# Neighbourhood and windowed attention in float32 halves: the low key product on 64 rows, scores of both heads of a tile in one step

## The chip, the cores and the metric

The program runs on 1 core of one Trainium2 chip. The metric is the device time of one execution in microseconds (us), taken as the median over runs. Engines are named as in the profile: PE is TensorE's matmuls, PEld its weight loads, DVE is VectorE, ACT is ScalarE, POOL is GpSimd, SP is SyncE, which issues most transfers.

## The reference, cut to what matters

One encoder layer over 2048 tokens of width 1024: normalise, one input projection, two groups of attention heads, an output projection, a SwiGLU feed-forward part and a last norm. All is float32. The change touches the scores `q . k` of both groups:

```
# A: 8 heads, a query sees a window of 8 x 16 neighbours in a grid of 32 x 64 tokens
logits = einsum(qb, kb) * scale + bias ; masked ; softmax ; @ vb
# B: 8 query heads over 2 key heads, |q - k| <= 128, with a sink logit
logits = einsum(qb, kb) * scale ; masked ; softmax with sink ; @ vb
# a head has 64 dimensions, so a score is a sum over 64 products
```

## The kernel before

**Stages.** The stages follow each other on PE: the input projection, attention, the output projection with its norms ("mix"), and the feed-forward part.

**Halves.** PE multiplies operands of type float32r in one pass at reduced precision. Where full precision is wanted, the projection stores each of q and k as a high and a low float32r half (`stage_hi`, `stage_lo`, to `qk_scratch`), and a product takes high x high, low x high and high x low. A head's 64 dimensions fill only half of the 128 rows of PE's array. So `q_st` holds for each head e of a pair the high half of q on rows 0 to 63 and its low half on rows 64 to 127. `k_st[:, e, 0]` holds the high half of the keys twice, on both halves of the rows, and `k_st[:, e, 1]` the low half twice. One unit's scores are two matmuls into one PSUM bank: L985 gives (q_hi + q_lo) x k_hi, and L986 adds (q_hi + q_lo) x k_lo. Both use all 128 rows, and both load the same weights, `q_st[:, e, tile]`.

**Order.** Attention has 8 rounds, 4 of the neighbourhood kind ("near") and 4 of the window kind. A round is two heads over all 2048 queries. It has 16 tiles of 128 queries and 32 units, and unit u is head e = u % 2 of tile t = u // 2. Key columns of one unit: near tiles 384 (8 of 16 tiles) or 512 (the other 8); window tiles 384, and 256 for the first and last tile of a round. The order on each engine is written out by `stream`: in each step s every stage runs for unit s minus its lag, and what is listed first comes first in the step:

- PE: `score` (lag 0), `turn` (lag 5: 3 or 4 transposes of the probabilities, L997), `values` (lag 7: probabilities x values, L1017, for one tile after its odd unit in window rounds, for two tiles after every fourth unit in near rounds)
- DVE: `invert` (lag 2, L938), `shift` (lag 0: scores plus bias with the running minimum, out of PSUM, L932), `normalise` (lag 2, L945), `results` (L959, after every 8 units)
- ACT: `copy_turned` (lag 5, L906), `set_sinks`, `exp` (L884)

So on PE a step is: two score matmuls, three or four transposes, and in some steps a group of value matmuls. The scores have 4 PSUM banks (`SC_BUFS`): `score(u)` waits until `shift(u - 4)` has read the bank. The transposes and the scores address the array as 128 rows x 128 columns; each value matmul has 64 output columns (128\*64), and the two heads of a tile use the two column halves.

**Transfers.** SP's `advance` loads the next round's q, k and v in four blocks b, each when the round's units 0 to 8(b + 1) - 1 are scored, and stores the results between them. `load_q` (L727) issues 2 transfers for each block, `load_k` (L737) 4, `load_v` 1, `store` (L756) 1. Window rounds load k and v once, since all four rounds share them. The first round's q and k are loaded during the projection (`load_first_q`, `load_first_k`, one call for each step of the projection). GpSimd makes the biases of the next near round and, in the window rounds, scales and splits the output projection's weights (`make_bias`, `gpsimd`).

Of the kernel before, what the change touches and what calls it, by code (L numbers as in the profile page):

```python
# [29 lines left out]
F32R = mybir.dt.float32r  # L30

P = 128
BANK = 512
D = 1024
S = 2048
HD = 64
GW = 64
NAH, SWH, SWKV = 8, 8, 2
# [8 lines left out]
HEADS = 2 * NAH + SWH + SWKV  # L47
# [11 lines left out]
def project_phase(nc, x, g_mix, w_in, rpb, cos2, sin2, ident_in, zeros_in, qk_dram, v_near_dram, v_win_dram,  # L59
# [159 lines left out]
    def load_ahead(att, i):  # L219
# [8 lines left out]
        if i in (3, 4):  # L228
# [3 lines left out]
            att.load_first_q(i - 3)  # L232
        if 7 <= i < 11:
            sp.wait_ge(proj_done, done + 7)
            att.load_first_k(i - 7)
# [387 lines left out]
def attention_phase(nc, qk_dram, v_near_dram, v_win_dram, rel_dram, near_mask_in, win_mask_in, sink_in, ident_in, o_dram, mem,  # L623
# [17 lines left out]
    def sem(n):  # L641
        return nc.alloc_semaphore(f"att_{n}")

    q_st, k_st, v_sb, sn, pr, pt, pt_low, o_st = (mem.q_st, mem.k_st, mem.v_sb, mem.sn, mem.pr, mem.pt, mem.pt_low,
                                                  mem.o_st)
    negmax, total, rtotal = mem.att_stats
# [63 lines left out]
    def f32(ap):  # L710
        return ap.bitcast(F32)
# [8 lines left out]


    def load_q(kind, r, b):

        qs = slice(b * BANK, (b + 1) * BANK)
        pair = bass.ds(2 * r, 2) if kind.near else bass.ds(2 * NAH - NEAR_ROUNDS + r, 2, SWH // SWKV)
        for part in range(2):
            sp.dma_start(f32(q_st[part * HD:(part + 1) * HD, :, qs]), heads[part, :, pair, qs]) \  # L727
                .then_inc(q_in[b], 16)

    def load_k(kind, r, b):  # L730

        lo, hi = kind.portions[b]
        ks = slice(lo * kind.unit, hi * kind.unit)
        pair = bass.ds(NAH + 2 * r, 2) if kind.near else slice(2 * NAH + SWH, HEADS)
        for part in range(2):
            for twice in range(2):
                sp.dma_start(f32(k_st[twice * HD:(twice + 1) * HD, :, part, ks]), heads[part, :, pair, ks]) \  # L737
                    .then_inc(k_in[b], 16)

# [31 lines left out]
    def load_first_q(part):  # L771

        pair = slice(0, 2)
        sp.dma_start(f32(q_st[part * HD:(part + 1) * HD, :, :]), heads[part, :, pair, :]).then_inc(q_in[0], 16)
        if part == 1:
            for b in range(1, 4):
                sp.sem_inc(q_in[b], 32)

    def load_first_k(piece):

        part, twice = piece // 2, piece % 2
        sp.dma_start(f32(k_st[twice * HD:(twice + 1) * HD, :, part, :]), heads[part, :, NAH:NAH + 2, :]) \
            .then_inc(k_in[0], 16)
        if piece == 3:
            for b in range(1, 4):
                sp.sem_inc(k_in[b], 64)

# [185 lines left out]
    def score(proj, kind, r, u):  # L973
        e, t = u % 2, u // 2
        b, n = t // 4, kind.chunks(t) * P
        if e == 0:
            if t % 4 == 0:
                pe.wait_ge(q_in[b], 32 * (r + 1))
            for i in kind.new_portions(t):
                pe.wait_ge(k_in[i], 64 * (r + 1) if kind.near else 64 * (NEAR_ROUNDS + 1))  # L980
        if isinstance(r, int) and r == 0 and u < SC_BUFS:
            proj.bank_free(pe, u)
        pe.wait_ge(shifted, UNITS * (r + 1) - SC_BUFS + u + 1)
        q, out = q_st[:, e, t * P:(t + 1) * P], sc[:, u % SC_BUFS, 0:n]
        pe.matmul(out, q, kind.keys(k_st[:, e, 0, :], t), start=True, stop=False)  # L985
        pe.matmul(out, q, kind.keys(k_st[:, e, 1, :], t), start=False, stop=True).then_inc(scored, 1)  # L986

# [48 lines left out]
class Memory:  # L1036
# [11 lines left out]
    def __init__(self, nc):  # L1048
# [8 lines left out]
        self.q_st = self.at("att_q_stack", 65536, [P, 2, S], F32R)  # L1057
        self.k_st = self.at("att_k_stack", 81920, [P, 2, 2, S], F32R)
        self.v_sb = self.at("att_values", 114688, [P, 32, P])
# [1164 lines left out]
```

## Time and profile before

| | us |
|---|---|
| median of 3 runs (2261.32 to 2263.62) | 2262.09 |
| the profiled execution's own time | 2259.97 |
| its span, from the first to the last instruction | 2258.2 |
| PE busy | 2208.8 (98% of the span) |
| PEld busy | 1818.5 (81%) |
| DVE busy | 1440.5 (64%) |
| ACT busy | 922.3 (41%) |
| POOL busy | 327.8 (15%) |

Matmuls are pipelined: each takes several times as long as the next one is behind it. A busy share of PE near 100% therefore only says that PE rarely stood with an empty array, and not that it works at its peak. What a matmul costs is read from the distance between the end of one and the end of the next. The granted TensorE clock is 0.996 of full speed on average. Attention takes the stretch from 442 to about 769 us; the last score matmul starts at 764 us.

### The profile page before, as it was taken

Reading aid. Unit: us, or ns where it says so; the run is one execution under the profiler, and the core shown is the slowest. Engines: PE = TensorE matmul, PEld = TensorE weight load, DVE = VectorE, ACT = ScalarE, POOL = GpSimd, SP = SyncE. Lnnn points to the kernel's source line nnn. Section 1 sums busy time; section 2 is a strip of 40 time slices with the busy share of each in tenths; the row PEclk is TensorE's granted clock in tenths of the full one; section 3 lists DMA queues with packets and bytes.
Section 4 is the critical chain, followed back from the end, with each engine's and each line's share of the span. In section 5 each row is a group of like instructions: output and inputs, shape, how many; then the busy total and the mean of one; then the engine's idle time right before and its main releaser. Section 6 shows DMA issues by size and latency. Waiting matters only on the chain.

```text
span 2258.2 us, 33189 instructions
## 1 busy us (share of the span) xinstructions
PE 2208.8 (98%) x11464; PEld 1818.5 (81%) x11464; DVE 1440.5 (64%) x2747; ACT 922.3 (41%) x1824; POOL 327.8 (15%) x304
## 2 busy tenths in 40 slices
PE   7999999999999999999999999999999999999998
PEld 6888888788877788778888887888888877888886
DVE  4412143399899777776666657665656578565776
ACT  4411121288888633343333334433333333131342
POOL 3370001145334100011212120000000002020100
PEclk9999999999999999999999999999999999999999
DMA  6472425789954275675545457323232286353544
GB/s 225 140 186 99 140 87 148 201 217 246 235 143 111 83 226 200 224 265 175 189 165 199 154 209 263 128 80 131 80 131 73 102 305 234 104 177 108 191 145 152
DMA packets 274677, 376.68 MB, mean 167 GB/s; under 512 B 15258, under 2 KB 182306, under 8 KB 269168
## 3 DMA queue, kind: packets, MB, share of 16 engines
q1 hardware_dynamic: 266528, 354.15, 49.3%
q0 software_dynamic: 5568, 11.87, 2.0%
q10 hardware_dynamic: 2448, 8.91, 1.4%
q8 instruction: 81, 1.33, 0.2%
q14 instruction: 52, 0.43, 0.1%
HBM read 237.77 MB, written 140.31 MB: 167 GB/s over the span
## 4 chain that ended last, share of the span: by engine, by line
PE 89%; DVE 6%; DMA 2%; issue 2%; ACT 1%; POOL 0%; DVEq 0%; ACTq 0%; SPq 0%
PE late_psum L2047 11%; PE late_psum L2048 11%; PE late_psum L2049 11%; PE late_psum L2078 6%; PE late_psum L2080 5%; PE late_psum L2079 5%; PE late_psum L1017 4%; PE late_psum L997 4%; PE late_psum L527 3%; PE late_psum L528 3%; PE late_psum L529 3%; PE late_psum L555 3%; PE late_psum L554 3%; PE late_psum L556 3%; PE late_psum L985 2%; PE late_psum L1396 2%
## 5 line engine op out<-in xcount | busy, mean ns | idle before, releaser
L2047 PE MATMUL late_psum<-ff_h,ff_ring 128*128 128x512 f32 x1232 | 479.9, 390 | 5.9 <-DVE ff_acts L1907 3.0
L2049 PE MATMUL late_psum<-ff_h,ff_ring 128*128 128x512 f32 x1232 | 479.3, 389 | 0.0
L2048 PE MATMUL late_psum<-ff_h,ff_ring 128*128 128x512 f32 x1232 | 479.3, 389 | 0.0
L2047 PEld LDWEIGHTS late_psum<-ff_h,ff_ring 128*128 128x128 f32 x1232 | 231.2, 188 | 55.9 <-DVE ff_h L1868 3.9
L2049 PEld LDWEIGHTS late_psum<-ff_h,ff_ring 128*128 128x128 f32 x1232 | 231.2, 188 | 48.1
L2048 PEld LDWEIGHTS late_psum<-ff_h,ff_ring 128*128 128x128 f32 x1232 | 231.2, 188 | 47.7
L2078 PE MATMUL late_psum<-ff_d,ff_a 128*128 128x512 f32 x616 | 240.6, 391 | 8.3 <-DVE ff_x L1967 5.3
L2079 PE MATMUL late_psum<-ff_d,ff_a 128*128 128x512 f32 x616 | 239.7, 389 | 0.0
L2080 PE MATMUL late_psum<-ff_d,ff_a 128*128 128x512 f32 x616 | 239.7, 389 | 0.0
L1967 DVE TENSOR_TENSOR ff_x<-late_psum,ff_x 128x512 f32<-128x512 f32 x224 | 153.6, 689 | 121.4 <-PE late_psum L2080 121.0
L1863 DVE TENSOR_TENSOR ff_ring<-ff_raw,ff_ring 128x512 fp32r<-128x512 f32 x176 | 127.5, 726 | 104.3 <-ACT ff_ring L1740 104.1
L884 ACT ACTIVATE att_probs<-att_neg_scores,att_negmax 128x385 f32<-128x385 f32 (+3 forms) x256 | 163.9, 640 | 27.4 <-DVE att_negmax L932 24.4
L1863 DVE TENSOR_TENSOR ff_ring<-ff_sums,ff_ring 128x512 fp32r<-128x512 f32 x132 | 96.4, 732 | 114.9 <-ACT ff_ring L1740 114.5
L1755 ACT CAST ff_a<-ff_a 128x768 fp32r<-128x768 f32 (+2 forms) x96 | 81.6, 879 | 209.6 <-DMA ff_a<-acts_scratch 209.6
L1740 ACT CAST ff_ring<-ff_raw 128x512 fp32r<-128x512 f32 x176 | 109.6, 624 | 140.8 <-PE late_psum L2049 137.6
L2078 PEld LDWEIGHTS late_psum<-ff_d,ff_a 128*128 128x128 f32 x616 | 115.6, 188 | 35.5 <-issue 4.3
L945 DVE TENSOR_SCALAR att_probs<-att_probs,att_rtotal 128x384 f32<-128x384 f32 (+2 forms) x256 | 143.5, 560 | 0.1
L1708 POOL TENSOR_TENSOR ff_d<-ff_d 128x1536 fp32r<-128x1536 f32 x9 | 35.7, 3962 | 727.7 <-ACT ff_d L1749 727.7
L997 PE MATMUL late_psum<-ident,att_probs 128*128 128x128 f32 x816 | 132.4, 275 | 7.1 <-DVE att_probs L945 3.0
L2080 PEld LDWEIGHTS late_psum<-ff_d,ff_a 128*128 128x128 f32 x616 | 115.6, 188 | 24.3
L2079 PEld LDWEIGHTS late_psum<-ff_d,ff_a 128*128 128x128 f32 x616 | 115.7, 188 | 23.6
L833 POOL TENSOR_TENSOR bias<-near_mask,rel 128x384 f32<-128x384 f32 (+1 forms) x72 | 84.9, 1213 | 319.6 <-DMA near_mask<-in_na_mask 198.0
(159 smaller groups left out, 4148.9 us busy)
## 6 DMA issues: line engine op xcount, KB each, us to landing
acts_scratch<-ff_acts SPq DMA_DIRECT2D x22, 1792.0 KB, 7.8
ff_a<-acts_scratch SPq DMA_DIRECT2D x24, 960.0 KB, 5.1
ff_raw<-in_w_gate SPq DMA_DIRECT2D x44, 512.0 KB, 3.8
ff_raw<-in_w_up SPq DMA_DIRECT2D x44, 512.0 KB, 3.9
ff_d<-down_scratch SPq DMA_DIRECT2D x21, 768.0 KB, 6.3
att_q_stack<-qk_scratch SPq DMA_DIRECT2D x56, 256.0 KB, 5.2
ffn_in_scratch<-mix_h_stage SPq DMA_DIRECT2D x8, 1792.0 KB, 6.2
ff_h<-ffn_in_scratch SPq DMA_DIRECT2D x14, 1024.0 KB, 7.6
```

The costliest lines, as they stand in the source:

```text
L884: nc.scalar.activation(pr[:, i, lo:hi], sn[:, i, lo:hi], ACT.Exp, bias=negmax[:, i:i + 1], scale=-1.0, accum_out=total[:, i:i + 1]).then_i ...
L945: nc.vector.tensor_scalar(pr[:, i, c0:c0 + n], pr[:, i, c0:c0 + n], rtotal[:, i:i + 1], None, ALU.mult).then_inc(probs_done, 1)
L997: last = pe.transpose(tp[:, u % 2, j * P:(j + 1) * P], pr[:, i, c0 + j * P:c0 + (j + 1) * P], ident[:])
L1740: nc.scalar.copy(ff.ring[m % TURNS][:, 0], weight_of(m)).then_inc(w_hi_done, 1)
L1863: nc.vector.tensor_tensor(ff.ring[m % TURNS][:, 1], weight_of(m), ff.ring[m % TURNS][:, 0], ALU.subtract) \
L1967: nc.vector.tensor_tensor(to, down_bank(e, j), to, ALU.add).then_inc(added, 1)
L2047: pe.matmul(out_bank, whi[:, k], hhi[:, :, k], start=(k == 0 and not onto), stop=False, skip_group_check=onto)
L2048: pe.matmul(out_bank, whi[:, k], hlo[:, :, k], start=False, stop=False, skip_group_check=onto)
L2049: last = pe.matmul(out_bank, wlo[:, k], hhi[:, :, k], start=False, stop=(k == 3), skip_group_check=onto)
L2078: pe.matmul(bank, hi, dhi, start=(i == 0 and not onto), stop=False, skip_group_check=onto)
L2079: pe.matmul(bank, hi, dlo, start=False, stop=False, skip_group_check=onto)
L2080: last = pe.matmul(bank, lo, dhi, start=False, stop=(i == n - 1), skip_group_check=onto)
```

## The change

The low half of the keys is stacked by head: `k_lo` holds it once, head 0 on rows 0 to 63 and head 1 on rows 64 to 127. The high half is kept twice as before, as `k_hi`. The q stack of head 1 is turned over (low half on rows 0 to 63, high half on rows 64 to 127), so that q's high half lies on the rows of that head's low keys (`half_of`). The low product is now q_hi x k_lo alone, on 64 rows; the product of the two low halves, which the 128-row matmul also gave, is dropped. `score` does nothing for odd units, and for an even unit issues four matmuls: high products of head 0 and head 1 (128 rows), then low products of head 0 (rows 0 to 63) and head 1 (rows 64 to 127), each pair of products into its own bank. It waits for `shift(u - 3)` where before it waited for `shift(u - 4)` and then, a step later, for `shift(u - 3)`. `load_q` issues 4 transfers of half the size for each block, `load_k` 3 in place of 4, and the first loads change in the same way.

```diff
--- before.py
+++ after.py
@@ -230,7 +230,7 @@
             for half in range(2):
                 sp.wait_ge(stored[half], 16 * QK_STEPS)
             att.load_first_q(i - 3)
-        if 7 <= i < 11:
+        if 7 <= i < 10:
             sp.wait_ge(proj_done, done + 7)
             att.load_first_k(i - 7)
         if 11 <= i < 15:
@@ -641,8 +641,8 @@
     def sem(n):
         return nc.alloc_semaphore(f"att_{n}")
 
-    q_st, k_st, v_sb, sn, pr, pt, pt_low, o_st = (mem.q_st, mem.k_st, mem.v_sb, mem.sn, mem.pr, mem.pt, mem.pt_low,
-                                                  mem.o_st)
+    q_st, k_hi, k_lo, v_sb, sn, pr, pt, pt_low, o_st = (mem.q_st, mem.k_hi, mem.k_lo, mem.v_sb, mem.sn, mem.pr, mem.pt,
+                                                        mem.pt_low, mem.o_st)
     negmax, total, rtotal = mem.att_stats
     win_mask, sinks, gcol, w_raw, ident, w_pool = mem.win_mask, mem.sinks, mem.gcol, mem.w_raw, mem.ident, mem.w_pool
     rel, masks, biases = mem.rel, mem.masks, mem.biases
@@ -719,23 +719,28 @@
 
 
 
+    def half_of(part, e):
+
+        row = (part + e) % 2 * HD
+        return slice(row, row + HD)
+
     def load_q(kind, r, b):
 
         qs = slice(b * BANK, (b + 1) * BANK)
-        pair = bass.ds(2 * r, 2) if kind.near else bass.ds(2 * NAH - NEAR_ROUNDS + r, 2, SWH // SWKV)
         for part in range(2):
-            sp.dma_start(f32(q_st[part * HD:(part + 1) * HD, :, qs]), heads[part, :, pair, qs]) \
-                .then_inc(q_in[b], 16)
+            for e in range(2):
+                head = bass.ds(2 * r + e, 1) if kind.near else bass.ds(2 * NAH - NEAR_ROUNDS + r + SWH // SWKV * e, 1)
+                sp.dma_start(f32(q_st[half_of(part, e), e:e + 1, qs]), heads[part, :, head, qs]).then_inc(q_in[b], 16)
 
     def load_k(kind, r, b):
 
         lo, hi = kind.portions[b]
         ks = slice(lo * kind.unit, hi * kind.unit)
         pair = bass.ds(NAH + 2 * r, 2) if kind.near else slice(2 * NAH + SWH, HEADS)
-        for part in range(2):
-            for twice in range(2):
-                sp.dma_start(f32(k_st[twice * HD:(twice + 1) * HD, :, part, ks]), heads[part, :, pair, ks]) \
-                    .then_inc(k_in[b], 16)
+        both = bass.ds((NAH + 2 * r) * HD, P) if kind.near else slice((2 * NAH + SWH) * HD, HEADS * HD)
+        for twice in range(2):
+            sp.dma_start(f32(k_hi[twice * HD:(twice + 1) * HD, :, ks]), heads[0, :, pair, ks]).then_inc(k_in[b], 16)
+        sp.dma_start(f32(k_lo[:, ks]), qk_dram[1, both, ks]).then_inc(k_in[b], 16)
 
     def load_v(kind, r, b):
         lo, hi = kind.portions[b]
@@ -770,20 +775,20 @@
 
     def load_first_q(part):
 
-        pair = slice(0, 2)
-        sp.dma_start(f32(q_st[part * HD:(part + 1) * HD, :, :]), heads[part, :, pair, :]).then_inc(q_in[0], 16)
+        for e in range(2):
+            sp.dma_start(f32(q_st[half_of(part, e), e, :]), heads[part, :, e, :]).then_inc(q_in[0], 16)
         if part == 1:
             for b in range(1, 4):
-                sp.sem_inc(q_in[b], 32)
+                sp.sem_inc(q_in[b], 64)
 
     def load_first_k(piece):
 
-        part, twice = piece // 2, piece % 2
-        sp.dma_start(f32(k_st[twice * HD:(twice + 1) * HD, :, part, :]), heads[part, :, NAH:NAH + 2, :]) \
-            .then_inc(k_in[0], 16)
-        if piece == 3:
-            for b in range(1, 4):
-                sp.sem_inc(k_in[b], 64)
+        if piece < 2:
+            sp.dma_start(f32(k_hi[piece * HD:(piece + 1) * HD, :, :]), heads[0, :, NAH:NAH + 2, :]).then_inc(k_in[0], 16)
+            return
+        sp.dma_start(f32(k_lo[:]), qk_dram[1, NAH * HD:(NAH + 2) * HD, :]).then_inc(k_in[0], 16)
+        for b in range(1, 4):
+            sp.sem_inc(k_in[b], 48)
 
     def load_first_v(b):
         load_v(NEAR, 0, b)
@@ -971,19 +976,25 @@
                {1: proj.last_low}, {UNITS + NORM_LAG - 1: lambda: mix.o_low(0)})
 
     def score(proj, kind, r, u):
-        e, t = u % 2, u // 2
+
+        if u % 2:
+            return
+        t = u // 2
         b, n = t // 4, kind.chunks(t) * P
-        if e == 0:
-            if t % 4 == 0:
-                pe.wait_ge(q_in[b], 32 * (r + 1))
-            for i in kind.new_portions(t):
-                pe.wait_ge(k_in[i], 64 * (r + 1) if kind.near else 64 * (NEAR_ROUNDS + 1))
+        if t % 4 == 0:
+            pe.wait_ge(q_in[b], 64 * (r + 1))
+        for i in kind.new_portions(t):
+            pe.wait_ge(k_in[i], 48 * (r + 1) if kind.near else 48 * (NEAR_ROUNDS + 1))
         if isinstance(r, int) and r == 0 and u < SC_BUFS:
             proj.bank_free(pe, u)
-        pe.wait_ge(shifted, UNITS * (r + 1) - SC_BUFS + u + 1)
-        q, out = q_st[:, e, t * P:(t + 1) * P], sc[:, u % SC_BUFS, 0:n]
-        pe.matmul(out, q, kind.keys(k_st[:, e, 0, :], t), start=True, stop=False)
-        pe.matmul(out, q, kind.keys(k_st[:, e, 1, :], t), start=False, stop=True).then_inc(scored, 1)
+            proj.bank_free(pe, u + 1)
+        pe.wait_ge(shifted, UNITS * (r + 1) - SC_BUFS + u + 2)
+        q, out = [q_st[:, e, t * P:(t + 1) * P] for e in range(2)], [sc[:, (u + e) % SC_BUFS, 0:n] for e in range(2)]
+        for e in range(2):
+            pe.matmul(out[e], q[e], kind.keys(k_hi[:, e, :], t), start=True, stop=False)
+        for e in range(2):
+            rows = half_of(0, e)
+            pe.matmul(out[e], q[e][rows], kind.keys(k_lo[rows], t), start=False, stop=True).then_inc(scored, 1)
 
     def turn(proj, kind, r, u):
         i, t = u % SN_BUFS, u // 2
@@ -1055,7 +1066,8 @@
         self.biases = [self.at(f"bias{i}", off, [P, 2, 3, w]) for i, off, w in ((0, 16896, 384), (1, 28672, 512), (2, 40960, 384))]
         self.pt_low = self.at("att_probs_turned_low", 54784, [P, 4, BANK])
         self.q_st = self.at("att_q_stack", 65536, [P, 2, S], F32R)
-        self.k_st = self.at("att_k_stack", 81920, [P, 2, 2, S], F32R)
+        self.k_hi = self.at("att_k_high", 81920, [P, 2, S], F32R)
+        self.k_lo = self.at("att_k_low", 98304, [P, S], F32R)
         self.v_sb = self.at("att_values", 114688, [P, 32, P])
         self.sn = self.at("att_neg_scores", 131072, [P, 8, BANK])
         self.pr = self.at("att_probs", 147456, [P, 8, BANK])
```

## Rows read from the trace of the kernel before

**Rows 1.** Busy us by stage: PE, PEld, DVE, ACT, POOL; clock, DMA share, GB/s.

```profile
450.00:606.00 156.00, 152.83 (x1447) 127.17 (x1448) 143.69 (x495) 137.10 (x360) 74.43 (x65) 0.98 0.98 237
606.00:766.00 160.00, 156.45 (x1467) 127.18 (x1463) 152.19 (x554) 138.07 (x438) 56.80 (x34) 1.00 0.45 120
766.00:2258.20 1492.20, 1464.97 (x6548) 1208.74 (x6546) 1004.56 (x1407) 537.62 (x834) 102.46 (x53) 1.00 0.49 169
```

**Rows 2.** Groups by line and shape, 442 to 767 us, PE.

```profile
L985 PE MATMUL late_psum<-att_k_stack,att_q_stack 128*128 128x384 f32 x176 | 76.5, 435 | 0.0
...
L985 PE MATMUL late_psum<-att_k_stack,att_q_stack 128*128 128x512 f32 x64 | 31.2, 488 | 0.0
...
L985 PE MATMUL late_psum<-att_k_stack,att_q_stack 128*128 128x256 f32 x16 | 6.0, 373 | 0.0
```

**Rows 3.** Timeline of PE in a window round: start us, us.

```profile
681.09 0.45 PE L985 MATMUL late_psum<-att_k_stack,att_q_stack 128*128 128x384 f32 x1
...
681.55 0.49 PE L997 MATMUL late_psum<-ident,att_probs 128*128 128x128 f32 x3
681.80 0.42 PE L985 MATMUL late_psum<-att_k_stack,att_q_stack 128*128 128x384 f32 x1
682.05 0.34 PE L986 MATMUL late_psum<-att_k_stack,att_q_stack 128*128 128x384 f32 x1
682.23 0.49 PE L997 MATMUL late_psum<-ident,att_probs 128*128 128x128 f32 x3
682.65 0.88 PE L1017 MATMUL late_psum<-att_probs_turned,att_values 128*64 128x128 f32 x12
683.45 0.45 PE L985 MATMUL late_psum<-att_k_stack,att_q_stack 128*128 128x384 f32 x1
```

**Rows 4.** Timeline of PEld, the same stretch; in brackets its idle time before.

```profile
682.65 0.64 PEld L1017 LDWEIGHTS late_psum<-att_probs_turned,att_values 128*64 128x64 f32 x12 [0.17 <-issue]
```

**Rows 5.** Timeline of PE after the last scores.

```profile
766.90 0.88 PE L1017 MATMUL late_psum<-att_probs_turned,att_values 128*64 128x128 f32 x12
767.71 0.44 PE L997 MATMUL late_psum<-ident,att_probs 128*128 128x128 f32 x2
```

**Rows 6.** Waits from 442 to 767 us: total us, times, longest.

```profile
PEld late_psum L997 <- issue: 9.7, 25, 0.8
...
PEld late_psum L997 <- DVE att_probs L945: 4.7, 10, 1.1
```

**Rows 7.** Timeline of PE in a near round.

```profile
520.87 0.63 PE L997 MATMUL late_psum<-ident,att_probs 128*128 128x128 f32 x4
521.43 1.97 PE L1017 MATMUL late_psum<-att_probs_turned,att_values 128*64 128x128 f32 x32
...
525.88 0.34 PE L986 MATMUL late_psum<-att_k_stack,att_q_stack 128*128 128x384 f32 x1
526.31 0.52 PE L997 MATMUL late_psum<-ident,att_probs 128*128 128x128 f32 x3
```

**Rows 8.** Timeline of DVE in a window round.

```profile
682.96 0.15 DVE L938 RECIPROCAL att_rtotal<-att_total 128x1 f32<-128x1 f32 x1
...
683.56 0.41 DVE L945 TENSOR_SCALAR att_probs<-att_probs,att_rtotal 128x384 f32<-128x384 f32 x1
683.89 0.15 DVE L938 RECIPROCAL att_rtotal<-att_total 128x1 f32<-128x1 f32 x1
```

**Rows 9.** Timeline of DVE, a little earlier.

```profile
680.07 1.45 DVE L945 TENSOR_SCALAR att_probs<-att_probs,att_rtotal 128x384 f32<-128x384 f32 x1
681.44 0.68 DVE L959 COPY att_o_stage<-late_psum 128x512 f32<-128x512 f32 x1
```

**Rows 10.** Timeline of POOL, the same stretch.

```profile
678.88 2.42 POOL L874 TENSOR_TENSOR w_pool<-att_w_out_raw,w_pool 128x1024 fp32r<-128x1024 f32 x1 [4.13 <-DVE att_negmax L932]
```

**Rows 11.** SP's own waits from 442 to 767 us.

```profile
SPq L756 <- DVE att_o_stage L959: 135.4, 30, 8.7
```

**Rows 12.** The transfers of L727: duration in ns, min/median/max.

```profile
L727 SPq DMA_DIRECT2D att_q_stack<-qk_scratch x56: 598/620/2580, 465.3 to 730.3; - x56
```

## The prediction

> **What bounds the kernel now.** I read four views in this order.
>
> The busy time by stage comes first. Attention's two main stretches, 450:606 (near rounds) and 606:766 (window rounds), have PE busy for 152.8 of 156 us and 156.5 of 160 us; DVE is close behind with 143.7 and 152.2 us [rows 1]. So two engines are candidates, and their work has to be compared for each tile. The change touches nothing outside attention (the rest, from 766 us on, is the same code), and attention must end before the output projection can, so what attention gains or loses is what the kernel gains or loses.
>
> The PE timeline of a window round gives the price of each piece. Ends are start plus duration, and the distance of two ends is what the second costs. A 384-column score matmul ends 0.18 us after what is before it, and the second 0.17 us after the first (682.04, 682.22, 682.39): 0.175 us each. Three transposes end 0.33 us later, so 0.11 us each [rows 3]. A group of value matmuls is different. Twelve of them (3 key chunks, 2 heads, each product as two instructions) end at 683.53, 0.81 us after the transposes [rows 3]; 32 of them end at 523.40, 1.90 us after the transposes before [rows 7]. The ten further pairs thus took 1.09 us, 0.109 us a pair, which is what one transpose takes alone: the two heads' products on the two column halves run side by side. Six pairs at 0.109 are 0.65 us, so 0.15 us of the 0.81 belongs to no product. Likewise the score matmul behind the values ends 0.37 us after them (683.90) where 0.175 is its own: 0.195 us more [rows 3]. Both extras come where the shape on the array changes between 128\*128 and 128\*64, and in both the weight load, which elsewhere runs ahead under the matmul before, stood idle for 0.17 us first [rows 4] (that row is the way in; the way out repeats it). A visit to the other shape costs 0.345 us. One window tile adds up: 4 x 0.175 + 6 x 0.11 + 0.65 + 0.345 = 2.36 us, exactly the distance from 681.09 to 683.45 [rows 3]. PE's stream is full there.
>
> DVE takes 0.93 us for a unit (682.96 to 683.89) [rows 8], so 1.86 us a tile, and about 0.17 us more for its share of `results`, my estimate from 0.68 us in every fourth tile [rows 9]: 2.03 us. Undisturbed it has room beside 2.36. It is disturbed: the same normalisation takes 0.41 us alone [rows 8] and 1.45 us [rows 9] while POOL works from 678.88 to 681.30 [rows 10]. Then PE waits for DVE. Transposes waited 35 times, with the weight load idle for 14.4 us [rows 6]. In one of these, the transpose comes 0.43 us after the low product's start [rows 7], where 0.18 us is usual (682.05 to 682.23) [rows 3]: a stall of 0.25 us where the load was idle for 0.38 us. Taking 0.13 us off each of 35 leaves about 10 us of stall in all attention. PE's stream is the bound, DVE the next one, 10 us of stalls lie between.
>
> **The change part by part.** There are 128 tiles: 88 with 384 columns, 32 with 512, 8 with 256 (two matmuls of this line for each tile) [rows 2].
>
> *One matmul less per tile.* If the two 64-row products run side by side, as the two column halves do, each tile saves one score matmul. The mean durations are 373, 435 and 488 ns for 256, 384 and 512 columns [rows 2], 0.058 us for each 128 columns; with 0.175 us for 384 that makes 0.117, 0.175 and 0.233. Saved: 88 x 0.175 + 32 x 0.233 + 8 x 0.117 = 23.8 us. No row shows two products on different rows. The bounds: 23.8 us if they overlap wholly, 0 if they run one after the other. I take 23.8, by the nearest row, the column pairs.
>
> *Two changes of shape more per tile.* The order in an even step becomes high, high (128 rows), low, low (64 rows), transposes (128 rows). PE goes to 64 rows and comes back once for each tile. No row shows this change either; the nearest is the change of columns. Entering with a float32r weight load is like the way from values to scores, +0.195 us; leaving to a transpose is like the way from transposes to values, +0.15 us. Together 0.345 x 128 = 44.2 us. From below: 0, if the array needs no pause for rows. From above I have no row with more than 0.345. I take the whole, since the pause has the same form both in and out, with three different neighbours, whereas the transposes of ordinary shape pay nothing extra behind score matmuls (0.33 us for three) [rows 3].
>
> The Trainium skill, page TensorEngine Tiling (Array Packing), section Tiling Modes, says that a change of tiling mode, not just of tile, drains TensorE, and lists row tilings as modes beside column tilings. It speaks against this change and agrees with the pause of the rows; it has no price. By a price of nothing the sum would be the no-pause rival's below; by the rows' price it is mine.
>
> *Another neighbour behind the values.* Odd steps no longer begin with scores, and values always fall in even steps (lag 7, after odd units). So transposes follow the values. That costs 0.37 us for two transposes (767.78 to 768.15) [rows 5], 0.15 us beyond 2 x 0.11, where the way to a score matmul cost 0.195. There are 64 such groups in window rounds and 32 in near rounds: 96 x 0.045 = 4.3 us saved.
>
> *The waits.* `score` now needs `shift(u - 3)` at once. Behind it on PE stand the step's transposes, which need normalise(u - 5), made by DVE in its step u - 3 just after that shift. So the wait comes some 0.4 us ahead of one that is there anyway, and four score matmuls lie between the two now. Both heads' scores come together, later for head 0 by about one high product and a pause, some 0.4 us, and earlier for head 1. DVE can be two units further behind before PE's next transposes wait. I cost this at nothing: it is hidden by DVE's 0.33 us of room per tile. If DVE had no such room, PE would pay up to the 0.4 us in a disturbed tile.
>
> *Stalls given back.* A tile of 384 columns goes from 2.36 to 2.36 - 0.175 + 0.345 - 0.045 = 2.49 us on PE, while DVE needs 2.03 us plus POOL's disturbance. A longer tile gives DVE time to catch up, and the stalls average 10 / 35 = 0.29 us, about two tiles' added time. Between 0 and 10 us of them vanish; I take 6.
>
> *Transfers and queues.* SP issues 2 transfers more for each q block at 0.62 us [rows 12], 1.2 us, and one less for k. Behind them on SP stand the value load and the store. SP waits there for DVE's results 30 times, 135 us in all [rows 11], which covers the extra 1.2 us; blocks are needed a round later, some 40 us. Were that cover gone, a late store would hold up `results` on DVE by up to 1.2 us for each block, 32 times. The keys' bytes fall by a quarter in near rounds, where the transfer engines are 0.98 busy [rows 1], but nothing on PE waits for keys now. Nothing either way. POOL's queue is unchanged. The first loads lie under the projection.
>
> *Sum.* -23.8 + 44.2 - 4.3 - 6 = +10.1 us. Profiled execution: 2259.97 + 10.1 = 2270. The median lies 2.1 us above the profiled time, so 2272 for the median.
>
> **The rivals.**
>
> *No pause for rows (faster).* PE's work falls by 23.8 + 4.3 = 28 us. The place is the two borders of the low pair; the price there is zero instead of 0.345 us. For it speaks only that no row shows this change; against it, every change of shape the trace has. PE would then need 316 - 10 - 28 = 278 us for 450:766, and DVE, busy for 295.9 of 316 us [rows 1], becomes the bound. DVE caps the gain at 20 us, and with stalls on both sides I take 14: 2248, between 2242 and 2254. The sign turns where a round trip costs 28 / 128 = 0.22 us, before stalls.
>
> The Trainium skill, page TensorE: Matmul & The Clock Gate, Part 3, says that weight loads for another row group are pulled ahead and that products on different row groups start some 4 ns apart. If that held across the change from 128 to 64 rows as well, it would give this rival's time; no run here shows it yet.
>
> *A cheaper pause.* The row change costs about half of the column change, 0.17 us: -23.8 - 4.3 + 22 = -6, with the stalls as they are or somewhat more: 2256 to 2262. Nothing in the trace speaks for it but the lack of a row.
>
> *The low products do not overlap (the change does not do what it says).* The pauses are paid and the matmul is not saved, or only the weight load of the second comes 0.11 us behind the first. Between 128 x 0.11 = 14 us and 23.8 us are added to mine, less the rest of the stalls: 2284 to 2294. For it: the value pairs overlap on different columns, and rows are another direction.
>
> *As mine, but no stall is given back, or the earlier wait makes new ones:* 2276 to 2282. It belongs to my forecast's range.
>
> **How the numbers follow.** Mine with its range 2266 to 2282: 0.60. Products that do not overlap: 0.13. Cheaper pause: 0.12. No pause: 0.15. The likeliest gives 2272. The range 2249 to 2285 takes in mine, the cheaper pause, about half of the no-pause case and the lowest edge of the products that do not overlap; it leaves out somewhat under 0.2. A change within 0.2% (4.5 us) is what a measurement of this kernel cannot tell from none. Faster (below 2257.6): no pause, and a fifth of the cheaper pause, 0.17. Same (to 2266.6): the rest of the cheaper pause and a little of mine, 0.13. Slower: 0.70.
>
> **What would show it.** The PE timeline of a window round: two high products 0.175 us apart; the first low product's end about 0.37 us behind, with the weight load idle for some 0.17 us before it; the second low product within 0.01 us of the first; transposes ending 0.26 us later for the first and 0.11 us for each further. Tiles about 2.49 us apart. Fewer waits of transposes for DVE. Attention's end at about 779 us in place of 769. Wrong would be: weight loads of the low pair that start under the high products (no pause), or a second low product that ends 0.11 us or more behind the first.

## The result, and the profile after

| | us |
|---|---|
| before, median of 7 runs (2258.50 to 2263.62) | 2261.32 |
| after, median of 7 runs (2266.36 to 2269.88) | 2268.03 |
| ratio after / before, 95% interval | 1.0029 (1.0018 to 1.0040) |
| the profiled execution after: time / span | 2268.03 / 2266.2 |

The change costs 6.7 us, with the interval 4 to 9 us. Slower was forecast, at 2272 us with a range of 2249 to 2285.

The extra time lies in attention. The first score matmul starts at 442.0 us before and at 440.5 after; the first product of the output projection starts at 769.7 and at 774.7. That is 327.6 us against 334.2, 6.6 us longer.

The busy time by stage after (window; PE, PEld, DVE, ACT, POOL; clock, DMA share, GB/s) answers to [rows 1]:

```profile
450.00:606.00 156.00, 155.29 (x1424) 113.67 (x1425) 139.89 (x488) 134.59 (x350) 73.31 (x65) 0.98 0.81 209
606.00:766.00 160.00, 160.00 (x1432) 111.27 (x1431) 150.59 (x544) 138.91 (x429) 56.75 (x34) 1.00 0.41 119
```

PE is busy for the whole of the window rounds (156.5 of 160 us before), and gets through fewer matmuls in the same 160 us: 1432 against 1467. DVE's share fell a little. A fuller PE that does less is what pauses between matmuls look like: a matmul's recorded duration covers its latency, so an array that empties and fills counts as busy.

The timeline of PE in a window round shows the price (start, duration), to be set beside [rows 3]:

```profile
711.89 0.44 PE L997 MATMUL late_psum<-att_k_low,att_q_stack 64*128 64x384 f32 x2
712.27 0.55 PE L1008 MATMUL late_psum<-ident,att_probs 128*128 128x128 f32 x3
712.74 0.88 PE L1028 MATMUL late_psum<-att_probs_turned,att_values 128*64 128x128 f32 x12
713.55 0.55 PE L1008 MATMUL late_psum<-ident,att_probs 128*128 128x128 f32 x3
713.85 0.60 PE L994 MATMUL late_psum<-att_k_high,att_q_stack 128*128 128x384 f32 x2
714.38 0.45 PE L997 MATMUL late_psum<-att_k_low,att_q_stack 64*128 64x384 f32 x2
714.76 0.55 PE L1008 MATMUL late_psum<-ident,att_probs 128*128 128x128 f32 x3
```

Read by ends. The two high products end at 714.45, 0.35 us after the transposes (714.10): 0.175 us each, without a pause. The low pair ends at 714.83, 0.38 us later, where a single 384-column product takes 0.175. The next three transposes end at 715.31, 0.48 us later, where three in line take 0.33. So going to 64 rows costs about 0.20 us and coming back 0.15. Behind the values (713.62) three transposes also take 0.48 us, 0.15 of it pause. A tile is 0.35 + 0.38 + 0.48 + 0.81 + 0.48 = 2.50 us; the two low pairs end 2.50 us apart (712.33, 714.83), against 2.36 us a tile before [rows 3].

The weight loads of the same stretch (in brackets the idle time before) answer to [rows 4]:

```profile
711.34 0.30 PEld L994 LDWEIGHTS late_psum<-att_k_high,att_q_stack 128*128 128x128 f32 x2
711.89 0.19 PEld L997 LDWEIGHTS late_psum<-att_k_low,att_q_stack 64*128 64x128 f32 x2 [0.25 <-issue]
712.26 0.31 PEld L1008 LDWEIGHTS late_psum<-ident,att_probs 128*128 128x128 f32 x3 [0.19 <-issue]
712.74 0.63 PEld L1028 LDWEIGHTS late_psum<-att_probs_turned,att_values 128*64 128x64 f32 x12 [0.17 <-issue]
713.55 0.31 PEld L1008 LDWEIGHTS late_psum<-ident,att_probs 128*128 128x128 f32 x3 [0.17 <-issue]
```

There are four idle stretches of the load for each tile, one at each change of shape, where there were two. The two loads of the low pair together take 0.19 us, hardly more than one: they go to different rows at the same time, and so do the products.

The waits of the transposes from 442 to 775 us (total us, times, longest), to be set beside [rows 6]:

```profile
PEld late_psum L1008 <- issue: 31.1, 157, 0.6
PEld late_psum L1008 <- DVE att_probs L950: 9.8, 55, 0.2
```

The counts have grown, since every pause is now a gap in the loads. The weight loads' longest wait laid to DVE was 1.1 us and is 0.2 us, which is no more than a pause.

The ends of all matmuls of attention say it more exactly. The distance of two ends is nearly constant for each kind of neighbours, so what goes beyond the median of its kind is a stall (counted from 0.03 us on, and not inside the groups of value matmuls). From 459 us to the last transposes the stalls add up to 10.5 us before, 4.5 in the near rounds and 6.0 in the window rounds. After the change there is none in that stretch. The medians also give the pauses over all tiles. The way into the low pair costs 0.193 to 0.196 us, for 256, 384 and 512 columns alike, and the way out 0.150 to 0.153 us. The second low product ends 0.003 to 0.004 us behind the first.

The first microseconds of attention are different. There the granted clock was low, before (first row) and after (second row):

```profile
446.00:457.00 11.00, 8.19 (x37) 6.84 (x37) 9.69 (x35) 8.60 (x23) 3.45 (x3) 0.69 0.56 158
446.00:457.00 11.00, 9.79 (x35) 6.36 (x34) 8.38 (x34) 8.56 (x22) 2.49 (x3) 0.50 0.61 173
```

After the change it stood at 0.50, the level of 1.2 GHz, for the whole stretch; PE had been idle for 4.1 us just before. Up to 459 us the matmuls lost 5.0 us against their usual distances, with the wait for the first probabilities, where they lost 4.3 us before. Added up, -23.8 (one product less) + 44.2 (two pauses more) - 4.3 (another neighbour) - 10.5 (stalls) + 0.7 (this start) gives +6.3 us, against the 6.6 us read above.

### The profile page after: what moved, and what is told of

It is laid out like the page before. It is cut to its first block, busy times and chain, and to the rows that moved or that the text cites. A ratio compares the mean times of both kernels' runs of the same rounds, so it can differ in the third digit from the quotient of the medians.

```text
span 2266.2 us, 33226 instructions
## 1 busy us (share of the span) xinstructions
PE 2223.7 (98%) x11464; PEld 1794.4 (79%) x11464; DVE 1442.4 (64%) x2747; ACT 925.7 (41%) x1824; POOL 325.0 (14%) x304
## 4 chain that ended last, share of the span: by engine, by line
PE 92%; DVE 4%; DMA 2%; ACT 1%; issue 1%; POOL 0%; SPq 0%; DVEq 0%; ACTq 0%
PE late_psum L2059 12%; PE late_psum L2060 12%; PE late_psum L2061 12%; PE late_psum L2090 6%; PE late_psum L2091 6%; PE late_psum L2092 6%; PE late_psum L1008 5%; PE late_psum L1028 5%; PE late_psum L555 3%; PE late_psum L554 3%; PE late_psum L556 3%; PE late_psum L527 3%; PE late_psum L528 3%; PE late_psum L529 3%; PE late_psum L1408 2%; PE late_psum L997 2%
## 5 line engine op out<-in xcount | busy, mean ns | idle before, releaser
L1008 PE MATMUL late_psum<-ident,att_probs 128*128 128x128 f32 x816 | 139.3, 290 | 1.6 <-DVE att_probs L950 1.2
```

What stands on the lines that cost most here:

```text
L1008: last = pe.transpose(tp[:, u % 2, j * P:(j + 1) * P], pr[:, i, c0 + j * P:c0 + (j + 1) * P], ident[:])
```

## The experiments

All times are medians; a ratio is to the kernel before on the same chip, with its 95% interval. For comparisons between kernels I use the ratios.

### The order alone

The kernel before with the changed order, on 128 rows throughout:

```diff
-        e, t = u % 2, u // 2
+        if u % 2:
+            return
+        t = u // 2
...
-        pe.wait_ge(shifted, UNITS * (r + 1) - SC_BUFS + u + 1)
-        q, out = q_st[:, e, t * P:(t + 1) * P], sc[:, u % SC_BUFS, 0:n]
-        pe.matmul(out, q, kind.keys(k_st[:, e, 0, :], t), start=True, stop=False)
-        pe.matmul(out, q, kind.keys(k_st[:, e, 1, :], t), start=False, stop=True).then_inc(scored, 1)
+        pe.wait_ge(shifted, UNITS * (r + 1) - SC_BUFS + u + 2)
+        q, out = [q_st[:, e, t * P:(t + 1) * P] for e in range(2)], [sc[:, (u + e) % SC_BUFS, 0:n] for e in range(2)]
+        for e in range(2):
+            pe.matmul(out[e], q[e], kind.keys(k_st[:, e, 0, :], t), start=True, stop=False)
+        for e in range(2):
+            pe.matmul(out[e], q[e], kind.keys(k_st[:, e, 1, :], t), start=False, stop=True).then_inc(scored, 1)
```

> The kernel before with the order of the change alone: both heads' scores in one even step (high, high, low, low), all on 128 rows, keys stacked as before. Every theory: 96 groups of values are followed by transposes and not by scores, 4.3 us less on PE, no pause more. They part on where the 10 us of stalls went that are gone after the change. Theory A, a longer tile lets DVE catch up: here the tile is 0.045 us shorter, so most of the stalls stay, 2257 us. Theory B, the new order itself gives DVE two units more of room: most of them are gone here too, 2248 to 2251 us. Rival to the whole pause account (the time of the change comes from the joint order, its stricter wait or the bunched scores, not from the array's shape): this kernel is slower than before, 2264 us or more.

Measured: 2253.48 us, ratio 0.9964 (0.9950 to 0.9978). It was run a second time beside other kernels:

> The first experiment's kernel once more, beside the next two on one chip. The gain of the order alone stands: ratio to before 0.995 to 0.998, 2250 to 2256 us.

Measured: 2254.94 us, ratio 0.9969 (0.9958 to 0.9980).

So half of the change is a gain of 7 to 8 us, and the 64-row products have to answer for the whole loss and for this gain too: 1.0029 - 0.9966 is 0.63%, 14 us. Of the two theories on the stalls neither holds alone. The work saved is 4.3 us, so the order itself removed 3 to 4 us of stalls, and not all 10. The waits of the repeated run's profile, 442 to 767 us:

```profile
PEld late_psum L1002 <- issue: 18.3, 85, 0.6
PEld late_psum L1002 <- DVE att_probs L945: 4.3, 25, 0.2
...
PE late_psum L1002 <- DVE att_probs L945: 1.4, 1, 1.4
```

With 96 pauses of 0.17 us ahead of transposes (16 us of these 22.6), about 6 us of idle loads remain. By the ends of the matmuls, counted as above, 5.5 us of stalls are left in the first profile of this kernel and 6.3 us in the second, of 10.5. So the order alone removed 4 to 5 us of them, and attention is 8.6 and 8.1 us shorter than before in these two profiles.

### Low products on the same rows

The changed kernel, but both heads' low products on rows 0 to 63:

```diff
-        row = (part + e) % 2 * HD
+        row = part * HD
...
-        sp.dma_start(f32(k_lo[:, ks]), qk_dram[1, both, ks]).then_inc(k_in[b], 16)
+        sp.dma_start(f32(k_lo[0:HD, :, ks]), heads[1, :, pair, ks]).then_inc(k_in[b], 16)
...
-            pe.matmul(out[e], q[e][rows], kind.keys(k_lo[rows], t), start=False, stop=True).then_inc(scored, 1)
+            pe.matmul(out[e], q[e][rows], kind.keys(k_lo[rows, e, :], t), start=False, stop=True).then_inc(scored, 1)
```

> The changed kernel with both heads' low products on rows 0 to 63 (low keys on 64 rows for both heads, q not turned over): same shapes and pauses, but nothing can overlap. If the row pair runs side by side in the changed kernel, as its ends 3 ns apart say, this one costs a score matmul more for each tile: 23.8 us, 2292 us. If two products on 64 rows overlap in part anyway, only the second's weight load shows, 0.11 us x 128 = 14 us, 2282 us. Rival, the overlap gave nothing and the modelled ends mislead: 2268 us.

Measured: 2294.27 us, ratio 1.0141 (1.0122 to 1.0159). Against the changed kernel that is 1.12% or 25 us, where 23.8 was expected. PE and weight loads of a tile:

```profile
701.19 0.60 PE L994 MATMUL late_psum<-att_k_high,att_q_stack 128*128 128x384 f32 x2
701.72 0.61 PE L997 MATMUL late_psum<-att_k_low,att_q_stack 64*128 64x384 f32 x2
```

```profile
701.72 0.29 PEld L997 LDWEIGHTS late_psum<-att_k_low,att_q_stack 64*128 64x128 f32 x2 [0.25 <-issue]
```

The low pair now ends 0.54 us after the high pair (701.79, 702.33) in place of 0.38, and its two loads take 0.29 us in place of 0.19. The overlap in the changed kernel is real, and it is worth one whole matmul a tile. As in the changed kernel, no stall is left here once the clock is full.

### Four changes of shape for each tile

The changed kernel in the order high 0, low 0, high 1, low 1:

```diff
         for e in range(2):
             pe.matmul(out[e], q[e], kind.keys(k_hi[:, e, :], t), start=True, stop=False)
-        for e in range(2):
             rows = half_of(0, e)
             pe.matmul(out[e], q[e][rows], kind.keys(k_lo[rows], t), start=False, stop=True).then_inc(scored, 1)
```

> The changed kernel in the order high 0, low 0, high 1, low 1: four changes of shape for each tile in place of two, and no overlap of the low products. Pause theory: 128 x 0.345 = 44 us and 23.8 us more than the changed kernel, 2336 us. Rival, the cost is one of being in the step at all and not of the change of shape: the lost overlap alone, 2292 us.

Measured: 2344.92 us, ratio 1.0365 (1.0346 to 1.0384), 3.36% or 76 us above the changed kernel; 68 were expected, and the rival's 24 is out.

```profile
691.00 0.55 PE L1007 MATMUL late_psum<-ident,att_probs 128*128 128x128 f32 x3
691.30 0.42 PE L994 MATMUL late_psum<-att_k_high,att_q_stack 128*128 128x384 f32 x1
691.66 0.44 PE L996 MATMUL late_psum<-att_k_low,att_q_stack 64*128 64x384 f32 x1
692.03 0.44 PE L994 MATMUL late_psum<-att_k_high,att_q_stack 128*128 128x384 f32 x1
692.40 0.44 PE L996 MATMUL late_psum<-att_k_low,att_q_stack 64*128 64x384 f32 x1
```

The ends are 691.55, 691.72, 692.10, 692.47, 692.84: after the first high product every step is 0.37 or 0.38 us for a product of 0.175. The 8 us beyond the expectation have their reason here: a way back that leads to a score matmul costs 0.195 us and not the 0.15 of a way to a transpose. Two more pauses at 0.195 make 0.39 a tile, 50 us, with 23.8 for the overlap 74 us.

### Low products first, directly behind the values

```diff
-        stream(pe, [(0, partial(score, proj)), (TURN_LAG, partial(turn, proj)), (PV_LAG, values)],
+        stream(pe, [(TURN_LAG, partial(turn, proj)), (PV_LAG, values), (0, partial(score, proj))],
```

and in `score` the low pair with `start=True` ahead of the high pair.

> The changed kernel with score last in the step and the low products first, so that values (128 rows x 64 columns) are followed directly by the low pair (64 rows x 128 columns) and the pair by the high products. Pause theory: a change between two special shapes costs one pause and not two, so 96 round trips lose 0.15 us each, 14.4 us less than the changed kernel's 2268, so 2254 us, or 2254 to 2260 if some stalls of DVE come back with the shorter tile. Rival, each special group costs its two pauses wherever it stands: 2268 us.

Measured: 2321.43 us, ratio 1.0258 (1.0244 to 1.0272). Neither answer: 52 us slower than the changed kernel. The pauses did what the theory said. In the timeline the low pair ends at 741.45, 0.31 us behind the values (741.14), and 0.12 of it is the 256-column product; so going straight from one special shape to the other costs one pause of about 0.19 us:

```profile
740.26 0.88 PE L1028 MATMUL late_psum<-att_probs_turned,att_values 128*64 128x128 f32 x12
741.07 0.38 PE L995 MATMUL late_psum<-att_k_low,att_q_stack 64*128 64x256 f32 x2
741.38 0.50 PE L997 MATMUL late_psum<-att_k_high,att_q_stack 128*128 128x256 f32 x2
741.72 0.49 PE L1008 MATMUL late_psum<-ident,att_probs 128*128 128x128 f32 x3
743.00 0.52 PE L1008 MATMUL late_psum<-ident,att_probs 128*128 128x128 f32 x3 [0.79 <-DVE att_probs L950]
```

What I had not seen is in the last row. With the scores last in the step, the transposes of the even and of the odd unit of a tile follow them at once, with no values between. They need DVE's last two units, which DVE began only when the scores before arrived. The engines take turns waiting: in the same stretch DVE stands for 1.37 us, until the score pair before this one ends at 739.68,

```profile
739.68 0.62 DVE L937 CUSTOM_DVE_ANT_0 att_neg_scores<-late_psum,att_win_mask,att_neg_scores 128x384 f32<-128x384 f32 x1 [1.37 <-issue]
```

and over attention PE's transposes wait for DVE and ACT:

```profile
PEld late_psum L1008 <- DVE att_probs L950: 36.6, 46, 1.5
PEld late_psum L1008 <- issue: 31.4, 64, 0.8
PE late_psum L1008 <- ACT att_probs_turned L911: 15.6, 31, 1.1
```

### The high products alone

The two low products are left out of `score`.

> The changed kernel without the two low products: a score is q x high keys alone, so its precision is lower; nothing else is left out. PE loses the two pauses and the low product, 68 us, against the changed kernel. If DVE is the next bound, as the no-pause rival of the prediction had it, the time stops near DVE's busy time of attention, 10 to 20 us below the kernel before: 2242 to 2252 us. If DVE's busy time is mostly waiting that shrinks with the load, PE counts further down: 2200 to 2225 us.

Measured: 2244.53 us, ratio 0.9923 (0.9905 to 0.9941), 17 us below before. PE lost 68 us of work against the changed kernel and the time only 24. DVE is full in the near and in the window rounds (third number after the comma):

```profile
450.00:606.00 156.00, 144.59 (x1441) 113.64 (x1442) 154.09 (x534) 144.96 (x395) 76.96 (x66) 0.98 0.91 226
606.00:746.00 140.00, 125.96 (x1179) 90.71 (x1180) 139.19 (x500) 121.64 (x390) 53.85 (x33) 1.00 0.41 118
```

With DVE's work as it is, a saving on PE gives back some 17 us here and no more, as the no-pause rival had it.

### The low keys loaded twice

The changed kernel with one more load of the low keys, into freed memory, awaited by `score`:

```diff
         sp.dma_start(f32(k_lo[:, ks]), qk_dram[1, both, ks]).then_inc(k_in[b], 16)
+        sp.dma_start(f32(mem.k_spare[:, ks]), qk_dram[1, both, ks]).then_inc(k_in[b], 16)
```

> The changed kernel with the low keys loaded a second time into 8 KB a partition that the change had freed, and score waits for both loads: the key bytes and transfers of the kernel before, and the longer q issue of the changed one. If the keys' bytes are hidden, as the prediction had it: 2268 us, within 2 us. Rival, the freed bytes gave something back in the near rounds, where the transfer engines were 0.98 busy: 2271 us or more.

Measured: 2271.07 us, ratio 1.0038 (1.0026 to 1.0050), against 1.0029 (1.0018 to 1.0040) for the changed kernel. The intervals overlap, so the medians decide nothing between the two expectations. The profile does: attention takes 333.5 us with the second load and 334.2 without, and there are no stalls in either once the clock is full. In these executions nothing on PE waited for the keys' bytes; the rest of the kernel, whose code is the same, took 3.4 us longer in this one.

### The transposes one unit later

`TURN_LAG` 6 in place of 5, in the order-alone kernel and in the kernel before:

```diff
-    TURN_LAG, PV_LAG, NORM_LAG = 5, 7, 2
+    TURN_LAG, PV_LAG, NORM_LAG = 6, 7, 2
```

> The order alone (first experiment, 2253.5 us) with the transposes one unit later (TURN_LAG 6 in place of 5), on PE and on ACT. No work changes; DVE gets one unit, 0.93 us, more room. If what is left of the stalls, some 6 us, is lack of room: 2247 to 2250 us. If DVE's disturbed stretches are longer than any such room, or the later transposes make ACT late with the next exp: 2253 us or more.

Measured: 2263.53 us, ratio 1.0009 (1.0000 to 1.0018).

> The kernel before with TURN_LAG 6 alone, order and products as they were. If room for DVE is what removed the stalls in the changed kernel and in the order alone, the same is to be had here: some 6 to 10 us less, 2252 to 2256 us. Rival, the stalls went because both heads' scores came in one step, and the lag does nothing: 2262 us.

Measured: 2291.01 us, ratio 1.0133 (1.0118 to 1.0149), 30 us slower. Both expectations missed. The waits of the second kernel, 450 to 790 us:

```profile
PEld late_psum L1017 <- issue: 22.3, 30, 1.5
...
PE late_psum L1017 <- ACT att_probs_turned L906: 19.8, 28, 1.3
PEld late_psum L1017 <- ACT att_probs_turned L906: 15.3, 43, 1.3
...
PEld late_psum L997 <- DVE att_probs L945: 5.3, 8, 1.7
PEld late_psum L997 <- issue: 4.9, 18, 0.5
```

The transposes (L997) do wait less, 10.2 us in place of 14.4 [rows 6]. But the values (L1017) now wait for ACT's copies of the transposed probabilities: between the transpose and the values that use it one unit is left where there were two. The stall moved to the next stage and grew there. With the joint order this costs 10 us (0.9966 to 1.0009), with the old order 30. That the joint order loses its 10 us in the same way is likely: there the values (L1022) wait for the copies as well, their loads for 8.8 us and the matmuls for 8.0 us.

### Head by head

The order alone, but high 0, low 0, high 1, low 1 in the joint step:

```diff
         for e in range(2):
             pe.matmul(out[e], q[e], kind.keys(k_st[:, e, 0, :], t), start=True, stop=False)
-        for e in range(2):
             pe.matmul(out[e], q[e], kind.keys(k_st[:, e, 1, :], t), start=False, stop=True).then_inc(scored, 1)
```

> As the order alone, but high 0, low 0, high 1, low 1 in the step, all on 128 rows. Head 0's scores reach DVE two matmuls, 0.35 us, sooner. If DVE's room counts in such amounts: 1 to 3 us below the order alone, 2250 us. If not: the same as it.

Measured: 2251.09 us, ratio 0.9956 (0.9943 to 0.9969). It is the fastest kernel with the full computation, 10 us below before. Against the order alone on the same chip (0.9958 to 0.9980) the intervals overlap, so that the earlier scores of head 0 help is likely and not shown. In the profiles attention is 1.1 us shorter than in the order alone's second profile (318.4 against 319.5 us), and the stalls are 4.1 us in place of 6.3.

### Less work on GpSimd

> The kernel before with GpSimd's work of the window rounds cut from 51 to 17 us: the output projection's weights are not scaled, and their low half is a second copy of them; the output is therefore another. If PE's stalls there come from DVE being held up while GpSimd works, the normalisation takes 0.41 us more often, the transposes wait less, and the time falls by most of the 5 us of stalls of the window rounds: 2256 to 2259 us. If GpSimd has nothing to do with them: 2261 us and waits as before.

```diff
-            nc.gpsimd.tensor_scalar(raw, raw, gcol[:, k:k + 1], None, ALU.mult).then_inc(w_scaled, 1)
+            pool.sem_inc(w_scaled, 1)
...
-            nc.gpsimd.tensor_tensor(w_lo, raw, w_hi, ALU.subtract).then_inc(w_lo_done, 1)
+            nc.gpsimd.tensor_copy(w_lo, raw).then_inc(w_lo_done, 1)
```

Measured: 2256.04 us, ratio 0.9976 (0.9966 to 0.9986), 5.4 us less, at the strong end of the expectation. DVE's normalisations from 606 to 766 us are busy for 57.65 us (136 of them) in this kernel and for 73.09 us (135) in the kernel before. The waits of the transposes in that stretch fell from 4.5 and 2.9 us (by DVE, and by "issue") to

```profile
PEld late_psum L997 <- issue: 1.4, 4, 0.6
PEld late_psum L997 <- DVE att_probs L945: 0.9, 2, 0.5
```

By the ends of the matmuls the stalls of the window rounds fell from 6.0 to 1.1 us, while those of the near rounds, where GpSimd's work was left alone, stayed at 4.5 us. So GpSimd's work in the window rounds, at work beside DVE, is the cause of most of the stalls there. For the near rounds, where GpSimd makes the biases, no run shows it.

## Why the prediction was right

**The bound.** Right. The two experiments that added work to PE on top of the changed kernel, where no stalls were left to take it up, lengthened the time by what was added (25 us for 23.8, 76 us for 74). The high products alone showed DVE as the next floor, 17 us down; the prediction capped the gain at 20.

**One matmul less per tile, 23.8 us.** Right: 25 us when the overlap was taken away by the same rows.

**Two changes of shape more, 44.2 us.** Right in both parts. The rows gave 0.20 us on the way in and 0.15 on the way back, and the medians over all tiles the same, for 0.195 and 0.15 forecast from the column changes. Four changes for each tile cost 76 us more, and 74 by these prices. The rule of the Trainium skill (TensorEngine Tiling (Array Packing), Tiling Modes), that a change of tiling mode drains TensorE, holds here for rows as for columns, for 0.15 to 0.20 us each.

**The rivals.** No pause, a cheaper pause, and low products that do not overlap are all excluded: the first by the weight load's idle time ahead of the low pair, the second by the pause of 0.20 us, the third by the same-rows experiment. The overlap that the Trainium skill, page TensorE: Matmul & The Clock Gate, Part 3, states for different row groups is there inside the pair, whose two loads take 0.19 us together. Across the change of shape the loads are not pulled ahead: the weight load stands idle for 0.25 us before the pair.

**Another neighbour behind the values, 4.3 us.** Right by its rows: 0.15 us of pause ahead of transposes (713.62 to 714.10 for three) in place of 0.195.

**The waits, costed at nothing.** Half right. The joint order did no harm, but it did good that I had not costed: some 4 us of stalls less by itself, as the order alone showed.

**Stalls given back, 6 of 10 us.** This is the mis-sized term. The 10 us were right (10.5 by the ends of the matmuls), but all of them went, and not 6. Some 4 to 5 us are the order's. The remaining 5.5 to 6.3 us went with the longer tile. No run has the longer tile without the joint order; but all four profiled kernels with both and the scores first in the step (the changed one, the same rows, four changes, the low keys twice) have no stall once the clock is full, and the order alone has. The start of attention, at the lower clock, took 0.7 us more, which no term had. The forecast of +10.1 became +6.7 for that reason, and the attention's end came at 774.7 us and not at the 779 that the prediction named. Of the 4 us between 2272 and 2268, 0.8 us come from the starting median (2262.09 then, 2261.32 over all runs). What the cause of the stalls is was argued from two rows and is now shown for the window rounds, by less work on GpSimd.

**Transfers and queues, nothing.** Not contradicted: with the low keys loaded twice attention took no longer. The medians alone would leave room for some microseconds.

## What to carry to other kernels

Products on half of the rows pay only when more work is in one visit than the two changes of shape cost. Here a visit costs 0.35 us and saved one matmul of 0.12 to 0.23 us; by these prices the low products of two tiles in one visit would just break even, which no run tried. Price such a change from any change of shape that the trace already has, by the distance of matmul ends, and count the visits.

When a change has two halves, run each alone: the reordering was worth 7 to 8 us, and it was hidden under the loss of the other half, 14 us. A later stage started one unit later to give its predecessor room takes that room from its successor; look at what stands next in the chain before moving a lag.

## What the runs showed of the hardware that was not expected

The pause at a change of shape is longer where the weight load behind it takes longer. Ahead of float32r loads of 128 columns it is 0.195 us, and of float32 loads 0.15 us; the loads themselves take 184 to 193 ns and 136 to 142 ns on average (groups by line and shape after, 450 to 772 us, mean ns after the comma):

```profile
L1008 PEld LDWEIGHTS late_psum<-ident,att_probs 128*128 128x128 f32 x812 | 86.1, 142 | 43.0 <-issue 30.4 <-DVE att_probs L950 9.8 <-DMA ident<-in_ident 1.6
L1028 PEld LDWEIGHTS late_psum<-att_probs_turned,att_values 128*64 128x64 f32 x1156 | 61.5, 136 | 13.1 <-issue 12.0 <-ACT att_probs_turned L911 1.0 <-DVE att_o_stage L964 0.2
L994 PEld LDWEIGHTS late_psum<-att_k_high,att_q_stack 128*128 128x128 f32 x250 | 38.3, 193 | 0.0
...
L997 PEld LDWEIGHTS late_psum<-att_k_low,att_q_stack 64*128 64x128 f32 x250 | 23.5, 184 | 34.7 <-issue 33.6
```

So the pause is about one weight load that can no longer hide under the matmul before. At half the clock both are longer. In this stretch of the kernel after, at 0.50 of full speed, the low pair ends 0.62 us behind its high pair (447.33, 447.95), and the next low pair 0.61 us behind its own (448.89, 449.50), where one product alone took 0.32 us:

```profile
446.34 0.99 PE L994 MATMUL late_psum<-att_k_high,att_q_stack 128*128 128x384 f32 x2
447.26 0.69 PE L997 MATMUL late_psum<-att_k_low,att_q_stack 64*128 64x384 f32 x2
447.88 1.01 PE L994 MATMUL late_psum<-att_k_high,att_q_stack 128*128 128x384 f32 x2
448.81 0.69 PE L997 MATMUL late_psum<-att_k_low,att_q_stack 64*128 64x384 f32 x2
```

The pause is 0.30 us there, and the median load of the low pair took 285 ns. This fits every change seen here, of rows and of columns, in and out, and straight from one to the other. The type of the operands changes together with the load's duration at a given clock, so that the load is the mechanism was not tried by itself.
